# Two of the 16 dots of each step in the dense blocks computed on TensorE instead of VectorE

## The reference

```
q = (h @ w_query);  s = q . sub_keys            # 8 heads, two halves of 128 keys
i1, i2 = top 16 of each half;  idx = top 16 of the 256 sums, as i1 * 128 + i2
wts = softmax(top 16 sums)
u = expert_u[idx]                               # per token and head: 16 rows of 2048
a = gelu(sum_d h[n, d] * u[n, h, k, d])         # the dots
out = sum_hk (a * wts)[n, h, k] * expert_v[idx[n, h, k]]
```

## Time and profile before

| | us |
|---|---|
| median of 3 runs (4700.55 to 4713.91) | 4706.99 |
| the profiled execution | 4705.42 |
| span of its trace | 4703.6 |
| dense blocks' dots, VectorE's entry to end of the last dot | 2908.2 to 3649.3 |
| one step of it (3101.3 to 3146.9) | 45.6 |
| from there to the start of the rows stage's products | 3649.3 to 3716 |
| rows stage and third block, to the end | 3716 to 4703.6 |

### The profile page before, as it was taken

How to read it: one execution, slowest core, us unless ns; L and a number is a source line. 1 busy time by engine, 2 the same in 40 slices (tenths; PEclk the granted TensorE clock), 3 DMA queues, 4 the chain that set the end, 5 groups by cost and what they waited for, 6 DMA issues and landing times.

```text
span 4703.6 us, 31737 instructions
## 1 busy us (share of the span) xinstructions
PE 3582.2 (76%) x10776; PEld 1650.1 (35%) x10776; DVE 2945.2 (63%) x3905; ACT 646.2 (14%) x1545; POOL 1521.1 (32%) x1102
## 2 busy tenths in 40 slices
PE   4879989999799899999999893000122799999892
PEld 0333434444344444444444341000111444444341
DVE  2322027988333302377768979999999856666568
ACT  0111001100132200111110110000455400000000
POOL 0000003543333100243443466556555222222224
PEclk7989999999899999999999897555555899999996
DMA  9998998999999889899999999999998799999997
GB/s 378 383 350 296 358 348 335 356 355 357 375 410 409 323 284 337 333 366 363 364 371 416 370 409 421 393 366 378 362 383 350 263 394 393 421 421 421 421 421 316
DMA packets 385245, 1736.67 MB, mean 369 GB/s; under 512 B 26432, under 2 KB 30048, under 8 KB 231248
## 3 DMA queue, kind: packets, MB, share of 16 engines
q0 software_dynamic: 150336, 1079.53, 57.1%
q1 hardware_dynamic: 234768, 655.39, 36.6%
HBM read 1703.00 MB, written 33.13 MB: 369 GB/s over the span
## 4 chain that ended last, share of the span: by engine, by line
PE 34%; DMA 29%; DVE 26%; issue 9%; ACT 1%; POOL 1%; SPq 0%; DVEq 0%; POOLq 0%; PEldq 0%; ACTq 0%
PE ps L938 25%; DVE big L2251 9%; DMA big<-in_peer_u,sel 5%; DMA big<-in_peer_v,sel 4%; DMA zone<-in_peer_u,sel 3%; DMA zone<-in_peer_v,sel 3%; DMA big<-in_w_in 3%; DVE activations L2286 2%; DMA big<-in_w_ada 2%; PE ps L1038 2%; DMA big<-in_peer_v,zone 2%; PE ps L1097 2%; DVE big L1907 2%; DVE big L1968 1%; DVE work L1822 1%
## 5 line engine op out<-in xcount | busy, mean ns | idle before, releaser
L938 PE MATMUL ps<-big,activations 128*128 128x512 f32 x4032 | 1768.5, 599 | 51.7 <-DMA big<-in_w_in 14.0
L938 PEld LDWEIGHTS ps<-big,activations 128*128 128x128 f32 x4032 | 766.2, 192 | 1036.5 <-issue 980.4
L910 POOL DMA_INDIRECT big<-in_peer_u,sel x256 | 413.9, 1617 | 312.2 <-DVE qts L2251 126.1
L1331 PE MATMUL ps<-ident,zt 128*128 128x128 f32 x3 | 0.9, 426 | 451.4 <-DVE zt L2225 451.4
L1968 DVE CUSTOM_DVE_ANT_0 big<-big 128x2048 f32<-128x2048 f32 x128 | 289.3, 2290 | 43.5 <-DMA big<-in_peer_u,sel 42.0
L884 POOL DMA_INDIRECT big<-in_peer_u,sel x128 | 217.8, 1701 | 285.4 <-DVE zone L1968 248.5
L1907 DVE SCALAR_TENSOR_TENSOR big<-big,work 128x2048 f32<-128x2048 f32 x115 | 270.5, 2352 | 62.7 <-DMA big<-in_peer_v,sel 59.3
L1897 DVE CUSTOM_DVE_ANT_0 big<-big 128x2048 f32<-128x2048 f32 x114 | 259.6, 2289 | 71.2 <-DMA big<-in_peer_u,sel 70.3
L2251 DVE CUSTOM_DVE_ANT_0 big<-big,zone 128x2048 f32<-128x2048 f32 x128 | 287.0, 2283 | 0.6 <-DVE activations L1929 0.2
L2251 DVE CUSTOM_DVE_ANT_0 big<-big,activations 128x2048 f32<-128x2048 f32 x128 | 287.0, 2283 | 0.4
L2286 DVE SCALAR_TENSOR_TENSOR activations<-big,work,activations 128x2048 f32<-128x2048 f32 x79 | 185.7, 2351 | 114.1 <-DMA big<-in_peer_v,sel 113.7
(11 more groups left out here) (268 smaller groups left out, 4420.3 us busy)
## 6 DMA issues: line engine op xcount, KB each, us to landing
big<-in_w_in SPq DMA_DIRECT2D x84, 2048.0 KB, 11.6
big<-in_w_ada SPq DMA_DIRECT2D x48, 2048.0 KB, 12.1
big<-in_w_out SPq DMA_DIRECT2D x24, 2048.0 KB, 12.0
big<-in_peer_w_query SPq DMA_DIRECT2D x24, 2048.0 KB, 10.1
misc<-in_peer_v SPq DMA_DIRECT2D x43, 1024.0 KB, 9.1
zt<-in_peer_v SPq DMA_DIRECT2D x43, 1024.0 KB, 9.2
zone<-in_peer_v SPq DMA_DIRECT2D x42, 1024.0 KB, 9.1
big<-in_w_branch_a SPq DMA_DIRECT2D x12, 2048.0 KB, 9.6
```

Of the source, the lines that this page charges most:

```text
L910: pool.indirect_dma_start(u_slot(m), None, eu, bass.IndirectOffsetOnAxis(ap=sel[:, t % 2, k:k + 1], axis=0)).then_inc(u_in[m % UR], 16)
L938: ins = nc.tensor.matmul(bank(bk), acts[:, k, b * P:(b + 1) * P], w[:, n % WS, k], start=(start and k == 0), stop=(stop and k == KT // 2 - 1))
```

## The change

Each step's dots k = 0 and 1 (`TURNED = 2`) no longer run on VectorE. GpSimd gathers their tiles first, into two tiles of their own (`turned_rows_at`, ring places 8 and 9 of before; the ring shrinks to `UR` = 8), after TensorE has transposed the tiles of the step before (`t_done`). TensorE transposes them in eight turns of 2 x 2 pieces of 128 x 128 (`turn_rows`), ScalarE copies each turn out of its bank (`rows_turned`, 128 x 512), and TensorE multiplies the transposed h of the block with it (`turned_products`, two products of 128 x 256 for each turn, all eight turns adding up in one bank). The diagonals of the resulting two 128 x 128 blocks are the dots; VectorE takes them one step later, before its third dot (`turned_dots`: a product with the identity and a sum). The hots of the first dense block are spread over turns 1, 2, 4, 5 and 7 of a step.

```diff
-UR = 10
+UR = 8
+TURNED = 2
+STEP_DOTS = TOPK - TURNED
+TURNS = KT // 2
...
+        turned_rows_at = (bg(8 * D, D), bg(9 * D, D))
...
             for t in range(STEPS_U):
                 pool.wait_ge(sel_ready, 2 * PH + t + 1)
                 scores_in(2 * PH + t + 1)
-                for k in range(TOPK):
-                    m = t * TOPK + k
+                if t == 0:
+                    pool.wait_ge(u_free, U_EARLY + 1)
+                pool.wait_ge(t_done, T_DOTS + t * TURNS)
+                for k in range(TURNED):
+                    pool.indirect_dma_start(turned_rows_at[k], ...).then_inc(rows_in, 16)
+                for k in range(TURNED, TOPK):
+                    m = t * STEP_DOTS + k - TURNED
                     pool.wait_ge(u_free, m + 1)
                     pool.indirect_dma_start(u_slot(m), ...).then_inc(u_in[m % UR], 16)
...
+            def turn_rows(t, j):
+                x = t * TURNS + j
+                if j == 0:
+                    pe.wait_ge(rows_in, 64 + 16 * TURNED * (t + 1))
+                pe.wait_ge(t_free, T_DOTS + x + 1)
+                for i in range(2):
+                    for k in range(TURNED):
+                        ins = nc.tensor.transpose(bank(4 + x % 4)[...], turned_rows_at[k][:, (2 * j + i) * P:(2 * j + i + 1) * P], ident[:, :])
+                ins.then_inc(t_done, 1)
+            def turned_products(t, j):
+                x = t * TURNS + j
+                pe.wait_ge(t_free, T_DOTS + x + 1 + 4)
+                ...
+                for i in range(2):
+                    ins = nc.tensor.matmul(products_bank(t), h_tile(t // PH, 2 * j + i), turned_tile(x)[...], ...)
+                ins.then_inc(turn_mul, 1)
...
+            for t in range(STEPS_U):
+                if t == PH + 1:
+                    turn_coefs(0)
+                for j in range(3):
+                    turn_rows(t, j)
+                for j in range(TURNS):
+                    turned_products(t, j)
+                    if j + 3 < TURNS:
+                        turn_rows(t, j + 3)
+                    for n in hots_behind(t, j):
+                        build(0, n)
...
             for t in range(STEPS_U):
-                top_exps(2 * PH + t + 1)
...
+                for j in range(TURNS):
+                    rows_turned(t, j)
+                    for n in hots_behind(t, j):
+                        hots_scalar(n)
+                        ...
+                    if j == 1:
+                        top_exps(2 * PH + t + 1)
...
+            def turned_dots(t):
+                dve.wait_ge(turn_mul, TURNS * (t + 1))
+                link(V.tensor_tensor(diag, products_bank(t)..., ident[:, :]..., ALU.mult))
+                V.tensor_reduce(pair_dots[b][:, h * TOPK:h * TOPK + TURNED], diag, AX.X, ALU.add).then_inc(turn_ok, 1)
...
-                for k in range(TOPK):
+                for k in range(TURNED, TOPK):
...
+                    if k == 4 and t:
+                        turned_dots(t - 1)
-                    for _ in range(4 if k < 10 else 64):
+                    for _ in range(4 if k < 12 else 64):
                         next(ahead, None)
```

More of the change, by code:

```diff
@@ L465, in hots_behind @@
             if PH < t < STEPS_U:
-                return [n for n in range(5 * (t - PH - 1), 5 * (t - PH)) if k == 0 and n < HOTS]
+                behind = (1, 2, 4, 5, 7)
+                n = 5 * (t - PH - 1) + behind.index(k) if k in behind else HOTS
+                return [n] if n < HOTS else []
             if t == STEPS_U:
@@ L921, in _ @@
                     elif turn < 2:
-                        pool.wait_ge(u_free, UR + PAIR * P - 8 + turn + 1)
+                        pool.wait_ge(t_done, T_DOTS + STEPS_U * TURNS)
+                    elif turn == 2:
+                        pool.wait_ge(turn_mul, STEPS_U * TURNS)
                     elif turn > 2:
@@ new lines, in turned_products @@
+            def turned_products(t, j):
+                x = t * TURNS + j
+                pe.wait_ge(t_free, T_DOTS + x + 1 + 4)
+                if j == 0 and t >= 2:
+                    pe.wait_ge(turn_ok, t - 1)
+                for i in range(2):
+                    ins = nc.tensor.matmul(products_bank(t), h_tile(t // PH, 2 * j + i), turned_tile(x)[:, i * TURNED * P:(i + 1) * TURNED * P],
+                                           start=(j == 0 and i == 0), stop=(j == TURNS - 1 and i == 1))
+                ins.then_inc(turn_mul, 1)
@@ L1327, in build_coefs, with turn_coefs @@
+            def turn_coefs(b):
                 pe.wait_ge(coef_ok, 2 + b)
-                if b:
-                    pe.wait_ge(coef_t_ok, 1 + b)
+                pe.wait_ge(c_ok, b * HOTS)
                 for j, src in enumerate((pair_dots[b], pair_ids[b][:, 0], pair_ids[b][:, 1])):
-                    ins = nc.tensor.transpose(bank(0)[:, j * P:(j + 1) * P], src, ident[:, :])
+                    ins = nc.tensor.transpose(bank(2)[:, j * P:(j + 1) * P], src, ident[:, :])
                 ins.then_inc(coef_tr, 1)
-                for n in range(HOTS):
-                    g = b * HOTS + n
-                    pe.wait_ge(hot_a, g + 1)
-                    if g >= 7:
-                        pe.wait_ge(c_ok, g - 6)
-                    for t in range(QUAD):
-                        ins = nc.tensor.matmul(bank(1 + g % 7)[:, t * P:(t + 1) * P], hot(g)[:, t, 1], hot(g)[:, t, 0], start=True, stop=True)
-                    ins.then_inc(built, 1)
@@ L1342, in _, with build @@
-            pe.wait_ge(mats, 4)
-            for b in range(PAIR):
-                build_coefs(b)
+            def build(b, n):
+                g = b * HOTS + n
+                pe.wait_ge(hot_a, g + 1)
+                if b and n < 7:
+                    pe.wait_ge(coef_t_ok, 3)
+                elif b:
+                    pe.wait_ge(c_ok, g - 6)
+                elif n >= 2:
+                    pe.wait_ge(c_ok, n - 1)
+                for t in range(QUAD):
+                    ins = nc.tensor.matmul(bank(built_bank(g))[:, t * P:(t + 1) * P], hot(g)[:, t, 1], hot(g)[:, t, 0], start=True, stop=True)
+                ins.then_inc(built, 1)
@@ new lines, in _ @@
+            pe.wait_ge(mats, 4)
+            for t in range(STEPS_U):
[9 more added lines that the diff above has]
+                        build(0, n)
+            turn_coefs(1)
+            for n in range(HOTS):
+                build(1, n)
@@ L2252, in _ @@
                                            accum_out=pair_dots[b][:, h * TOPK + k:h * TOPK + k + 1]).then_inc(u_free, 1)
[L2253 to L2254 removed]
+                if t == PH:
+                    pair_coefs(0)
+            turned_dots(STEPS_U - 1)
             def arrived_3(i):
```

63 lines of the change are left out of this document (45 added, 18 removed).

## The result

| | before | after |
|---|---|---|
| median (range) of 4 runs, us | 4706.49 (4700.55 to 4713.91) | 4661.19 (4657.15 to 4668.46) |
| ratio to before, 95% interval | | 0.9905 [0.9885, 0.9924] |
| span of the profiled execution | 4703.6 | 4655.3 |
| start of the span to VectorE's entry to the stage | 2908.2 | 2909.1 |
| the stage, to the first dot of `step_3` | 741.0 | 698.5 |

The changed kernel is 0.95% faster (0.76 to 1.15%); 0.8% was forecast, 4668 us with a range of 4655 to 4692. In lines of the changed kernel L2356 is a dot, L2336 and L2338 the new pair, L1937 the maximum that ScalarE waits for, L937 a turned gather, L941 one of the other 14, L1366 transposes, L1377 products with the turned h, L1400 a hot's products.

What follows compares the result with a forecast made beforehand. The prediction took VectorE to bound the stage: -56.8 us over 16 steps, +15 at the entry and +4 in hot steps give -37.8 us, so 4668 us against the median 4706.49, range 4655 to 4692.

Steps and rivals of the forecast that it cites:

- What bounds the kernel: Stage: VectorE busy 44.2 of 45.6 us a step; what leaves it moves the whole tail forward.
- Two dots less, and the diagonal: VectorE's step: -4.43 us for two dots, +0.88 for the diagonal pair; -3.55 a step, -56.8 for 16.
- DMA engines: Stage: a step's 16.9 MB take 40.1 us; busy share goes from 0.93 to 0.95, 2 us to spare.
- The rival in which they don't keep up: Gathers into 8 places at 390 instead of 421 GB/s: steps of 43.4 us, +22 us, 4690; chance 0.09.
- The issue of the gathers and the turning loop: GpSimd's queue and ScalarE-TensorE chain: last transposes at S + 26, first turned gather at S + 28.4; no cost.
- The hot steps: Steps 9 to 14: a hot delays the last transposes to S + 30.3 to 30.8; +4 us, bounds 0 and 20.
- what would take off up to 3 us: Hot steps: TensorE may be at 2.4 GHz in part of them, taking off up to 3 us.
- the 3 us to spare: Each step's first dot: its tile lands at S + 40.7, needed at S + 43.6; VectorE does not wait.
- The limit of 14 us: Turning loop: last transposes 14 us behind L1843 is where the slower-kernel rival decides; that rival 4700 to 4755, chance 0.09.
- The entry: VectorE's entry to the stage: turned gathers on old ring places wait for it; +15 us, bounds 10.5 and 17.
- The tail: Behind the stage: same bytes and order, gap and tail as long as before, 66 and 988 us.
- the rival recorded ahead of it: Rerun of the changed kernel: the 6.7 us shorter tail belongs to the change, again 1047 to 1048 us; no chance given.

Runs made afterwards that it cites:

- The kernel with 14 dots: Kernel before without dots k = 0 and 1 of each step and their gathers, nothing on TensorE instead: 4630.79 us, ratio 0.9849.
- second trace: The changed kernel run again unchanged, as base for the other experiments on its chip: 4661.7 us, ratio 0.9921.
- the early kernel: Changed kernel with the turned tiles on ring places 0 and 1, so their gathers go before VectorE enters: 4652.09 us, ratio 0.9901.
- ring of 8: Kernel before with a ring of 8 tiles instead of 10, nothing else: 4702.41 us, ratio 1.0001.
- spread kernel: Changed kernel, turned tiles on places 0 and 1, SyncE's loads in steps 2 to 4, their output in step 6: 4644.15 us, again 4645.09.

## Why the prediction was right

**What bounds the kernel** held: the stage is VectorE's, and what left it moved the tail forward. Of the span's -48.3 us the stage gave -42.5, the head +0.9, the tail -6.6.

**Two dots less, and the diagonal.** -3.65 us a step where -3.55 was said; the pair is 0.79, not 0.88, since the sum releases the next operation 0.34 us after its start and the product 0.45 after its own (I had 0.35 and 0.53). 16 steps give -58.4 instead of -56.8. The kernel with 14 dots shows 4.43 us for the dots alone in a plain step.

**DMA engines.** They fed it, with no wait of VectorE for a tile from step 2 on, at 405 GB/s in a step. Their share was 1.00, not the 0.95 forecast. That had been worked out as 40.1 of 42 us, while by the earlier trace rows the share is 0.93 at 372 GB/s already. The rival in which they don't keep up did not come.

**The issue of the gathers and the turning loop.** In the plain step above the first turned gather goes at 3088.84, S + 28.2 (S + 28.4 forecast). That of the first dot follows at 3092.67, S + 32.0 (S + 32.2), and its tile lands 8.8 us after that start, at S + 40.9 (S + 40.7), some 2.5 us before it is needed. The last transposes, though, are earlier than worked out. That gather, TensorE in that step, and its windows at the start of the burst and later in it:

```profile
3092.67 1.91 POOL L941 DMA_INDIRECT big<-in_peer_u,sel  x1 [0.30 <-issue]
...
3078.24 2.08 PE L1377 MATMUL ps<-big,activations 128*128 128x256 f32 x4 [14.84 <-ACT big L1724]
3080.11 1.06 PE L1366 MATMUL ps<-ident,big 128*128 128x128 f32 x4
...
3082.72 1.03 PE L1377 MATMUL ps<-big,activations 128*128 128x256 f32 x4
3083.59 0.60 PE L1366 MATMUL ps<-ident,big 128*128 128x128 f32 x4
...
3078.20:3081.20 3.00, 2.96 (x9) 2.50 (x10) 3.00 (x4) 0.96 (x2) 0.41 (x2) 0.50 1.02 423
3082.30:3086.80 4.50, 4.48 (x25) 3.67 (x23) 4.47 (x5) 1.20 (x2) 1.88 (x1) 1.00 1.01 419
```

After 14.8 us of waiting TensorE starts at a granted clock of 0.50 (1.2 GHz), and from 3082.3 on it is at 1.00 (2.4 GHz): two products (four records) take 2.08 us, then 1.03, four transposes 1.06, then 0.60. The transposes end 3084.19 - 3077.12 = 7.1 us behind the maximum, not 9.3. The prediction had taken 1.7 us for two products throughout, less than they take at the lower clock and more than at the higher.

**The hot steps** are where the sum was off: +4 us was taken, 0 came. Steps 9 to 14 are 41.92 to 42.28 us, like the others. One of them, with its maximum at 3413.32:

```profile
3414.44 2.08 PE L1377 MATMUL ps<-zone,misc 128*128 128x256 f32 x4 [8.12 <-ACT zone L1724]
...
3419.27 2.08 PE L1400 MATMUL ps<-zt 128*128 128x128 f32 x8 [1.91 <-ACT zt L1748]
...
3421.14 1.91 PE L1377 MATMUL ps<-zone,misc 128*128 128x256 f32 x4
3422.84 0.79 PE L1366 MATMUL ps<-ident,big 128*128 128x128 f32 x4
...
3423.47 1.03 PE L1377 MATMUL ps<-zone,misc 128*128 128x256 f32 x4
...
3424.34 0.60 PE L1366 MATMUL ps<-ident,big 128*128 128x128 f32 x4
...
3425.21 1.16 POOL L937 DMA_INDIRECT big<-in_peer_u,sel  x1 [0.47 <-PE ps L1366]
```

The hand-over to TensorE came after 5.95 us (6.1 forecast), the hot took 2.08 (2.1), and the two products and two groups of transposes behind it 3.6 instead of 5.4: again the clock rising within the burst (0.50 over the hot, 1.00 from 3423.5 on), which the prediction had named as what would take off up to 3 us. The transposes end 11.6 us behind the maximum and not 13.6 to 14.1, the gather is 0.2 us late, and no dot is missed. The term that was mis-sized is this chain, by 2 to 2.5 us. The changed kernel stands at the edge of a miss all the same: in its second trace two of the six steps have their last transposes 11.9 and 12.5 us behind, and the first dot's gather slips by a dot, at no wait of VectorE. That is the other half of the account: a miss is a whole dot, as the prediction has it, and the 3 us to spare were about right as well, but one whole miss is less than they are. The limit of 14 us for the last transposes fits roughly: no wait at 12.5, 0.47 us once at 12.6 (the early kernel), 0.8 to 1.6 us at 15.0.

**The entry**: 15.6 us, 15 forecast, by the mechanism given; with SyncE's loads held the wait was 10.06 us, where the prediction had 10.5 for the gathers alone. The parenthesis that late DMA work also eats the slack of step 1 came too, 0.45 us.

**The tail** was forecast as equal and is 6.6 us shorter. As far as the traces can tell this is scatter and not the change's doing. For the change speaks its second trace, 1048.0 us, which is what the rival recorded ahead of it asks for. Against it, the kernels with the tail's code of before have 1054.3, 1047.8 (ring of 8) and 1047.4 us (14 dots), the early one, with the code of after, has 1056.0, and two traces of the same spread kernel have 1047.6 and 1052.0. Which of the program's waits make this scatter was not looked into.

So of the 6.8 us between forecast and result, 4 are the hot steps and 1.6 the pair; the scatter of head and tail is as large as the rest.

## What to carry to other kernels

Where an engine is the bound of a stage, price the stage with its back-to-back operations removed and hand-overs added, and then follow each new chain against the moment at which its result is asked for: here the chain took 7 to 12 us, VectorE begins to wait somewhere between 12.5 and 15, and the kernel with the chain some 9 us longer was slower than before. When work is moved to other buffers, look at which of them is free first at the stage's entry; tiles on late places ahead of the queue, with three loads beside them, cost 13 to 15 us, a third of the gain. And in a queue that goes forward once for each operation of another engine, lateness comes in whole operations, and the items are best ordered by when each is needed: two gathers moved ahead of three made a third turned dot worth its while.

## What the runs showed of the hardware

A gather is issued in 0.94 us beside a back-to-back VectorE sum over 128x2048 (one operand, 128x1 written), and in 1.9 us, one for each operation, beside a dot of the same 128x2048 and the same duration (two operands, 128x2048 written). So when it has to wait for something else first, it comes late by whole dots: 15.5, 17.8, 20.0, 22.2, 24.4 or 26.6 us behind the maximum. The DMA engines' busy share reads 0.93 at 372 GB/s, 1.00 at 405 and 1.01 at 421, so it hardly tells the last two apart. Taking three one-tile loads out of a saturated entry did not shorten VectorE's waits (16.1 and 16.4 us); they only moved to later dots. And TensorE's clock rose from 0.50 to 1.00 inside bursts that follow waits of 8 to 15 us, so a chain of short bursts is priced with its first part at 1.2 GHz and its last at 2.4.
